# A hybrid decoder step: first tile's queries from PSUM, two of a tile's five low parts on VectorE

## The reference, cut to what matters

```python
def block(xb):                                     # xb: normalised tokens
    q = (xb @ w_query).reshape(PEER_BLOCK, PEER_HEADS, 2, PEER_HALF)      # 8 heads
    s = jnp.einsum('bhpd,phnd->bhpn', q, sub_keys)                        # 128 keys, twice
    top_s, top_i = lax.top_k(s, PEER_TOPK)                                # 16 of 128
    cand = top_s[:, :, 0, :, None] + top_s[:, :, 1, None, :]
    best_s, best_j = lax.top_k(cand.reshape(PEER_BLOCK, PEER_HEADS, PEER_TOPK * PEER_TOPK), PEER_TOPK)
    e1 = jnp.take_along_axis(top_i[:, :, 0, :], best_j // PEER_TOPK, axis=-1)
    e2 = jnp.take_along_axis(top_i[:, :, 1, :], best_j % PEER_TOPK, axis=-1)
    gate = jax.nn.softmax(best_s, axis=-1)
    u_sel = expert_u[e1 * PEER_NKEYS + e2]         # 128 experts of 16384 a token
    act = jax.nn.gelu(jnp.einsum('bd,bhkd->bhk', xb, u_sel), approximate=False)
    v_sel = expert_v[e1 * PEER_NKEYS + e2]
    return jnp.einsum('bhk,bhkd->bd', gate * act, v_sel)
```

## Time and profile before

| | |
|---|---|
| median of three timed runs | 3597.07 us |
| the profiled execution | 3595.11 us, its span 3593.4 us |
| PE busy | 3406.2 us (95%) |
| DVE busy | 2622.7 us (73%) |
| ACT busy | 1017.6 us |
| POOL busy | 1028.0 us |
| TensorE's mean granted clock | 0.968 |

### The profile page before, as it was taken

One profiled execution on the slowest core, in us unless ns is written; L12 is line 12 of the kernel. 1 busy time (PEld: TensorE's weight loads), 2 busy tenths in 40 slices (PEclk: granted clock), 3 DMA queues, 4 the chain that ended last, 5 costly groups with the idle time before them and its releaser, 6 DMA issues.

```text
span 3593.4 us, 57482 instructions
## 1 busy us (share of the span) xinstructions
PE 3406.2 (95%) x21552; PEld 3338.8 (93%) x21552; DVE 2622.7 (73%) x4997; ACT 1017.6 (28%) x1345; POOL 1028.0 (29%) x792
## 2 busy tenths in 40 slices
PE   6989999899998999998899899999999999999997
PEld 6989999879998999998898899999999999999996
DVE  5544344323343179999999899999999999999996
ACT  5742222121232133222454122222222222222222
POOL 0000000000000032222000555555555555555550
PEclk8999999889999999999999999999999999999998
DMA  2111111111232233332689989998999999999993
GB/s 106 35 34 37 47 39 37 49 47 47 90 111 67 89 111 113 103 97 87 194 266 266 362 322 337 331 326 319 325 330 328 336 329 324 323 324 328 332 321 111
DMA packets 304487, 699.12 MB, mean 195 GB/s; under 512 B 23872, under 2 KB 124224, under 8 KB 303328
## 3 DMA queue, kind: packets, MB, share of 16 engines
q0 software_dynamic: 98736, 363.50, 27.8%
q1 hardware_dynamic: 104112, 276.89, 22.8%
q10 hardware_dynamic: 101504, 56.89, 5.2%
HBM read 604.96 MB, written 92.22 MB: 194 GB/s over the span
## 4 chain that ended last, share of the span: by engine, by line
PE 75%; DVE 19%; DMA 2%; issue 1%; ACT 1%; DVEq 1%; ACTq 0%; SPq 0%; POOL 0%; PEldq 0%; POOLq 0%
PE PS L1429 28%; PE PS L366 16%; PE PS L1412 14%; PE PS L1144 7%; PE PS L1173 5%; DVE HOTG L1913 3%; DVE fold L1840 2%; PE PS L381 1%; DVE HOT L1909 1%; DVE HOT L1910 1%; DVE besti L1784 1%; DVE sc L1775 1%; DVE besti L1776 1%; PE PS L1352 1%; DVE best L1781 1%
## 5 line engine op out<-in xcount | busy, mean ns | idle before, releaser
L1429 PE MATMUL PS<-AH,VH 128*128 128x368 f32 x2048 | 514.9, 333 | 18.4 <-DVE AL L2014 12.6
L1429 PE MATMUL PS<-AH,VL 128*128 128x368 f32 x2048 | 515.9, 333 | 0.0
L710 POOL DMA_INDIRECT SLOT<-rows_u,EID x256 | 345.6, 1350 | 580.4 <-DMA GW<-gate_matrices 275.7
L1429 PE MATMUL PS<-AL,VH 128*128 128x368 f32 x2048 | 510.2, 330 | 0.0
L710 POOL DMA_INDIRECT SLOT<-rows_v,EID x256 | 334.4, 1306 | 204.9 <-DVE SLOT L1946 166.7
L1429 PEld LDWEIGHTS PS<-AH,VH 128*128 128x128 f32 x2048 | 366.0, 189 | 21.1 <-DVE AL L2014 13.8
L1429 PEld LDWEIGHTS PS<-AL,VH 128*128 128x128 f32 x2048 | 367.0, 189 | 0.0
L1429 PEld LDWEIGHTS PS<-AH,VL 128*128 128x128 f32 x2048 | 366.2, 189 | 0.0
L1955 DVE SCALAR_TENSOR_TENSOR XLF<-SLOT,GA,XLF 128x1024 f32<-128x1024 f32 x256 | 327.4, 1279 | 0.8 <-DMA SLOT<-rows_v,EID 0.5
L1030 ACT ACTIVATE VH<-VRAW 128x512 fp32r<-128x512 f32 x256 | 157.6, 628 | 565.0 <-PE PS L1429 565.0
L1946 DVE SCALAR_TENSOR_TENSOR SLOT<-SLOT,XHF 128x1024 f32<-128x1024 f32 x256 | 311.7, 1218 | 5.4 <-DMA SLOT<-rows_u,EID 5.1
(11 more groups left out here) (331 smaller groups left out, 6703.9 us busy)
## 6 DMA issues: line engine op xcount, KB each, us to landing
RAW<-experts_u SPq DMA_DIRECT2D x128, 512.0 KB, 6.1
VRAW<-experts_v SPq DMA_DIRECT2D x256, 256.0 KB, 5.8
gate_matrices<-stg ACTq DMA_DIRECT2D x22, 2048.0 KB, 10.3
GW<-gate_matrices SPq DMA_DIRECT2D x96, 384.0 KB, 6.9
RAW<-weights SPq DMA_DIRECT2D x69, 512.0 KB, 3.5
activations<-AS SPq DMA_DIRECT2D x64, 368.0 KB, 2.5
AS<-activations SPq DMA_DIRECT2D x64, 368.0 KB, 3.0
GW<-gate_matrices SPq DMA_DIRECT2D x32, 320.0 KB, 5.8
```

The source lines that it names most:

```text
L710: pool.indirect_dma_start(out=SLOT[n % NSLOT][:, :], out_offset=None, in_=table, in_offset=bass.IndirectOffsetOnAxis(ap=ids, axis=0)).then ...
L1429: mm = pe.matmul(PS[:, 4 + 2 * (d % 2) + t, 0:CH], w[:, d % 2, c * P:c * P + P], x[:, c, t * CH:t * CH + CH], start=(c == 0 and n == 0), s ...
```

## The change

1. `SEL_E`: tile 0 has 4 early blocks and tile 7 has 5 (before 5 and 4). The sum stays 44.
2. In the query projection ScalarE copies, for each of 8 heads, the first 128 columns from PSUM to `qst`, ahead of the copy to `qrow`. The first DMA into `qst` goes away.
3. TensorE transposes only `xtok(0)` first (into banks 6 and 7), then makes the scores of tile 0, then block 0. `xtok(1)` follows after block 2 and `XS` after block `FIRST_E[1]`, both by way of banks 0 and 1.
4. The zeroing of the two accumulators goes from VectorE to ScalarE (an activation with scale 0).
5. The low parts: of the blocks of tile i+1, the first two are made by VectorE in the lookups of tile i (after L1845 and after L1854). The others stay on GpSimd, and the first of these three now waits until VectorE has finished tile i. The DMA of the queries of tile i+1 stands behind that one.

```diff
-SEL_E = (5, 5, 5, 5, 5, 5, 5, 4, 5)
+SEL_E = (4, 5, 5, 5, 5, 5, 5, 5, 5)
...
-            for b in range(2):
-                pool.wait_ge(q_out[b], 16 * (HP // 2))
-            pool.dma_start(qst[:, :, :], q_dram[:, :, 0:P]).then_inc(qst_in, 16)
...
             def e_low(n, slot):
 
+                pool.wait_ge(e_lo, n)
                 pool.wait_ge(e_hi, n + 1)
...
+            e_low(0, 0)
             pool.iota(IOTA[:, :, :], pattern=[[1, NKEYS], [0, 2]], base=0, channel_multiplier=0,
                       allow_small_or_imprecise_dtypes=True).then_inc(iota_set, 1)
-            for n in range(PRE + 1):
+            for b in range(2):
+                pool.wait_ge(q_out[b], 16 * (HP // 2))
+            for n in range(1, PRE + 2):
                 e_low(n, n % 2)
             for i in range(NTILE):
-                e_low(FIRST_E[i] + 1, (FIRST_E[i] + 1) % 2)
+                if 0 < i <= NSP + 1:
+                    pool.wait_ge(sel_done, i + 1)
+                elif i:
+                    pool.wait_ge(sel_g, i - NSP - 1)
+                e_low(FIRST_E[i] + 2, FIRST_E[i] % 2)
                 if i + 1 < NTILE:
                     pool.wait_ge(sel_mm, i + 1)
...
-                for r in range(2, SEL_E[i] + 1):
+                for r in range(3, SEL_E[i]):
                     e_low(FIRST_E[i] + r, (FIRST_E[i] + r) % 2)
...
                 act.wait_ge(unit_done, filled(unit_of(n)))
+                act.activation(qst[:, j, :], PS[:, 3 * (n % 2), 0:P], ACT.Copy)
                 act.activation(thirds(qrow[:, j % 2, :]), pset(n % 2), ACT.Copy).then_inc(free_w, 1)
...
-            for b in range(NSP):
-                act.activation(xtok(b), wide(b), ACT.Copy).then_inc(tok_set, 1)
-            act.activation(XS, PS[:, 6:8, :].rearrange("p a (k t) -> p (a k) t", t=HALF), ACT.Copy).then_inc(tok_set, 1)
-            e_block(0, 0, 16)
+            act.activation(xtok(0), wide(3), ACT.Copy).then_inc(tok_set, 1)
             act.wait_ge(sel_mm, 1)
             sel_scores()
+            e_block(0, 0, 16)
             e_block(1, 1, 16)
...
                     e_block(n, n % 2, 16 * (n // 2 + 1))
+                    if r == 0 and i == 0:
+                        act.wait_ge(tok_mm, 2)
+                        act.activation(xtok(1), wide(0), ACT.Copy).then_inc(tok_set, 1)
+                        for b in range(NSP):
+                            act.activation(acc(b), C[:, 0:D].rearrange("p (k t) -> p k t", k=KD), ACT.Copy, scale=0.0
+                                           ).then_inc(tok_set, 1)
+                    if r == 0 and i == 1:
+                        act.wait_ge(tok_mm, 3)
+                        act.activation(XS, PS[:, 0:2, :].rearrange("p a (k t) -> p (a k) t", t=HALF), ACT.Copy
+                                       ).then_inc(tok_set, 1)
...
             pe.wait_ge(free_w, HP + 2)
             pe.drain().then_inc(e_mm, 2)
-            x_transposes()
+            x_transposes(0, 6)
+            sel_scores(0)
             e_block(0, 0)
-            pe.wait_ge(tok_set, NSP + 1)
-            sel_scores(0)
+            pe.wait_ge(tok_set, 1)
             e_block(1, 1)
...
+                    if r == 0 and i == 0:
+                        pe.wait_ge(sel_sc, 1)
+                        x_transposes(1, 0)
+                    if r == 0 and i == 1:
+                        pe.wait_ge(sel_sc, 2)
+                        half_transposes()
...
                 dve.tensor_tensor(hot[:, :, :, :], places(topf), names(startb), ALU.is_ge)
+                e_low(FIRST_E[i + 1])
                 dve.drain()
...
                 dve.tensor_tensor(hot[:, :, :, :], places(topf), names(iota_b), ALU.is_equal)
+                if i + 1 < NTILE:
+                    e_low(FIRST_E[i + 1] + 1)
                 dve.drain()
...
-            dve.wait_ge(tok_mm, 1)
-            for b in range(NSP):
-                dve.memset(acc(b), 0.0)
```

More of the change, by code:

```diff
@@ L1322, in sel_scores @@
             def sel_scores(n):
-                pe.wait_ge(qst_in, 16 * n + 32)
+                pe.wait_ge(qst_in, 16 * n + 16)
                 for h in range(HP):
@@ L1327, in sel_scores, with x_transposes, half_transposes @@
                 mm.then_inc(sel_mm, 1)
-            def x_transposes():
-                for b in range(NSP):
[L1333 to L1336, removed]
+            def x_transposes(b, at_bank):
+                for k in range(KD):
+                    out = PS[:, at_bank + k // 4, (k % 4) * P:(k % 4) * P + P]
+                    pe.matmul(out, XH[:, k, b * P:b * P + P].bitcast(F32), const("ident"), start=True, stop=False)
+                    mm = pe.matmul(out, XL[:, k, b * P:b * P + P].bitcast(F32), const("ident"), start=False, stop=True)
+                mm.then_inc(tok_mm, 1)
+            def half_transposes():
                 for k in range(KD):
                     for h in range(2):
-                        out = PS[h * HALF:h * HALF + HALF, 6 + k // 4, (k % 4) * P:(k % 4) * P + P]
+                        out = PS[h * HALF:h * HALF + HALF, k // 4, (k % 4) * P:(k % 4) * P + P]
                         for n, x in enumerate((XH, XL)):
@@ L1377, in _ @@
                         pe.wait_ge(sel_sc, i + 1)
+                        if i < 2:
+                            pe.wait_ge(tok_set, 2 + 3 * i)
                         if i - 1 > NSP:
@@ L1449, in flush_half @@
             def flush_half():
-                pe.wait_ge(tok_set, NSP + 2)
+                pe.wait_ge(tok_set, NSP + 4)
                 for k in range(KD):
@@ L1749, in _, with e_low @@
                 split_lo(dve, B_WQ + j + 2, (B_WQ + j + 1) % 2)
+            def e_low(m):
+                dve.wait_ge(e_lo, m)
+                dve.wait_ge(e_hi, m + 1)
+                dve.tensor_tensor(WL[:, m % 2, :], RAW[:, m % 2, :], WH[:, m % 2, :].bitcast(F32),
+                                  ALU.subtract).then_inc(e_lo, 1)
             def evict(i):
@@ L1962, in _ @@
                 s_gated(0, e)
-            dve.wait_ge(tok_set, NSP + 1)
+            dve.wait_ge(tok_set, NSP + 3)
             def group_dve(g, first=False, last=False):
@@ L2032, in group_dve @@
                     if last and d == 2:
-                        dve.wait_ge(tok_mm, 2)
+                        dve.wait_ge(tok_mm, 4)
                         for b in range(NSP):
```

9 lines of the change are left out of this document (3 added, 6 removed).

## The result

| | before | after |
|---|---|---|
| median of five timed runs | 3597.85 us | 3617.77 us |
| the profiled execution | 3595.11 us | 3618.53 us |
| VectorE's first tile | 1283.34 | 1270.44 |
| the gate matrices begin | 1724.81 | 1748.66 |

The changed kernel is slower: ratio 1.0053, 95% interval 1.0041 to 1.0064. (The median before of 3597.07, given further up, is of three of these five runs.) The prediction said 3617 us, in a range of 3602 to 3632, so the forecast case came in. The span grew by 23.4 us (3593.4 to 3616.8) and the gate matrices begin 23.85 later, so nothing behind this stage gave time back or took more.

The account below looks back on a forecast made before the run. TensorE and VectorE were both taken as close to the bound. 13 us late by tile 4, +7.6 in tiles 4 to 7 and +0.5 in tile 8 made 21 on 3595.1, forecast as a median of 3617 us, range 3602 to 3632.

Parts of the forecast that it names:

- Shift of the gate matrices = shift of the end: After the tiles: any shift of the gate matrices' start, 1724.81 before, was taken as an equal shift of the end.
- The copies of queries, 0.4: Query projection: eight 128-column copies on ScalarE were charged 0.4 us in all, bounds 0 and 2.5.
- Tile 0's start, 15.1 earlier: VectorE's first tile was to start at 1268.2, 15.1 us earlier than at 1283.34.
- The wait at the first low part, 23 us: Tile 0: VectorE was to stand 23 us at its first low part, for block 4's chain through TensorE and ScalarE.
- c: Time the granted clock costs TensorE's scores after idle time: between 0 and 2.5 us, taken as 1.2 a start.
- Tile 1: VectorE was to stall 6.6 us, after 3.2 us of TensorE idle time; tile 2 would start 10 us late.
- Tiles 2 and 3, 50 each: Same chain holds VectorE 2 to 4 us each: 50 us a tile against 48.1, 13 late at tile 4.
- Tiles 4 to 7, 51.9 each: Scores wait for the eviction, VectorE then for ScalarE's high part: 51.9 us a tile against 50.0, +7.6 for four.
- rival (b): TensorE's clock does not fall after idle time: sum about +8 or +5, 3602 us; chance 0.14.
- the clock that falls at every start: Rival: TensorE starts cold after each wait, 3.3 us more at 7 or 8 starts, 3630 us; chance 0.15.
- Low parts in VectorE's maxima hold nobody: GpSimd's low parts beside VectorE's maxima were assumed to hold neither engine; if they collided, 2 us a tile.
- Rival (c), faster, 3575: Collisions go and VectorE's low parts never wait: 44 us less at best, half if engines wait a little, 3575; chance 0.13.

Follow-up runs that it names:

- The early tile alone: Changed kernel with every low part on GpSimd and five blocks in tile 0, as before: 3580.07 us, ratio 0.9946; timed again 3579.07 us, ratio 0.9942.
- The filler matmuls: Changed kernel plus 14 unused 128-column matmuls on TensorE ahead of the scores of tiles 5 to 8: 3611.97 us, ratio 1.0031.
- the best kernel here: Changed kernel with low parts and block shares as before, and the exponential one early block later from tile 3 on: 3573.10 us, ratio 0.9925.

## Why the prediction was right

**Shift of the gate matrices = shift of the end.** It held: 23.85 and 23.4. Of the 23.85, the stage itself is 21.2, the predicted 21; the other 2.6 arise before it. Of these, 2.5 stand before ScalarE's first copy to `qrow` (1183.63 before, 1186.11 after), where the code is the same; in all profiled executions that copy began at 1182.82 to 1186.86, so I put them down to variation between runs. This also means that the median landing within 1 us of 3617 is better than the method deserves. The prediction's own working, 3595.1 + 21 and the 2 us to the median, gives 3618 and not 3617.

**The copies of queries, 0.4.** TensorE's waits for them grew from 1.36 to 1.53 and from 1.96 to 2.1 us: 0.3. From the first copy to `qrow` to the first transpose it was 74.9 us in the three kernels without the copies and 75.1 in the changed kernel's trace; of the nine others with them three show 75.1 and six 76.6. So the copies cost 0.2 here and can cost 1.7, within the bounds given.

**Tile 0's start, 15.1 earlier.** 12.9 by the clock, 15.5 against TensorE's first transpose (24.8 us from it before, 9.2 after).

**The wait at the first low part, 23 us.** 23.95, by the links that the prediction named: low part, queries, scores, block 4, Gelu, table, exponential, high part. The idle time of TensorE in it was 3.0 and not 4.1, and c was 1.6 (4.95 for the scores) and not 1.2. The early tile alone, which keeps the lead, shows that nothing else in the change eats it.

**Tile 1.** Predicted stall 6.6, measured 6.96; predicted idle time ahead of the scores 3.2, measured 2.66. Tile 1 took 51.9, predicted 51.3 (1336.0 + 1.2 to 1388.5).

**Tiles 2 and 3, 50 each.** 49.9 and 47.8: the second is 2 us shorter than I allowed. The lag at tile 4 is 13.7, of which 2.6 stood before the stage: 11.1, for a predicted 13.

**Tiles 4 to 7, 51.9 each.** 52.7. VectorE's first low part waited 7.0, 8.1, 6.9 and 3.7 us, where 4 to 7 were forecast. Here a term was mis-sized: c. I took 1.2 from two rows of the kernel before, in which 3.89 us of idle time cost 2.5 and 2.62 cost nothing. The same stretch has a third such row, which I did not read:

```profile
1588.18 5.38 PE L1325 MATMUL PS<-KEYS,qst 128*128 128x256 f32 x16 [2.28 <-issue]
1593.21 0.68 PE L1352 MATMUL PS<-XH,WH 128*128 128x368 f32 x2
```

Here 2.28 us of idle time, less than in the row that cost nothing, cost 1.7 (5.03 for the scores, granted clock 0.66). The mean of the three is 1.4, and rival (b)'s support, that idle times under 3 us cost nothing, was already gone. The filler matmuls measured 1.7 on the mean, and without them the tile would be 51.0, close to the 50.7 that the prediction gave for c = 0. With c = 1.7 its sum for the tile is 52.4. Tile 8, predicted 0.5 longer than before, was 0.7 shorter (49.2 for 49.9). So the errors, 1.9 us too much before tile 4, 3.3 too little in tiles 4 to 7 and 1.2 too much in tile 8, cancel: that the stage comes to 21.2 for a predicted 21 is in part luck.

The Trainium skill's rule of the clock that falls at every start ("TensorE: Matmul & The Clock Gate", "HAM oscillation — how this bites in real kernels") would give scores of 6.6 us each. The six rows of the changed kernel with over 2 us of idle time ahead say 4.95, 5.03, 5.03, 6.09, 4.84 and 3.35: the trace agrees in part, and the measurement decides at just under half of the rule's price, 1.5 of 3.3 us on the mean.

**Low parts in VectorE's maxima hold nobody.** They don't. The first maxima of tile 5 and the low part beside them, VectorE's first:

```profile
1541.31 3.18 DVE L1804 MAX8 best<-sc 128x8 f32<-128x128 f32 x16
...
1541.24 2.39 POOL L680 TENSOR_TENSOR WL<-RAW,WH 128x1024 fp32r<-128x1024 f32 x1 [19.65 <-DVE gate L1900]
```

The 16 maxima take 3.18 us together. One by one, a MAX8 of this shape takes 0.28 us (median), with a GpSimd instruction under way or without. And `pick<-hot,delta` (L1847 before, L1880 after) takes 1.22 or 1.23 in all nine tiles; before it took 3.21 to 3.27 in seven of them. Counting VectorE's single instructions of over 1.9 us, each of which had a low part beside it, gives 27 before and one after. This part of the change did what it says: 27 collisions of 2.0 us are 54, and the busy time shows 32.1 less with 20.8 of low parts added, which is 52.9. What it bought was spent at the waits.

**Rival (c), faster, 3575.** Its time is nearly that of the best kernel here, but by another way. It asked that TensorE finish block FIRST_E[i+1] - 2 within 26 us of the tile's start; in tile 4 it finished 34.6 us in (ScalarE goes on at 1523.22), where the forecast had 33.7. What the prediction did not price is that the first part of the change alone gives 20.6 us, nearly all of the 22 in (c).

## What to carry to other kernels

When two engines are both near their bound, count an instruction moved from one queue to another by what it must wait for, and not by its duration: here the move of 17 low parts of 1.23 us removed some 53 us of collisions and brought 68 us of waits. A lead on one engine is kept only as long as nothing in its queue is bound to the slower one, so test the parts of a change apart: the early start alone is worth 20.6 us, and was lost to a part that came with it. When a hand-written order places a short step (here an exponential), its best place depends on which engine leads at that point, tile by tile.

## What the runs showed of the hardware

```profile
1310.57 2.73 DVE L1868 TENSOR_TENSOR fold<-pick 128x1024 f16<-128x1024 f16 x1
...
1309.51 3.24 POOL L680 TENSOR_TENSOR WL<-RAW,WH 128x1024 fp32r<-128x1024 f32 x1 [8.08 <-ACT WH L955]
```

  The fold takes 0.69 alone and ends here at 1313.3, after the low part (1312.75). The low part itself takes 3.24 instead of 2.4: it came while VectorE's `pick` (1309.27 to 1310.5) was under way. This agrees with the Trainium skill, "SBUF — State Buffer", "SBUF: two separate sides", where whichever starts first holds the shared port for the whole instruction. MAX8 was not held (0.28 us with and without).
- TensorE's clock after a short idle time. In the kernel before, scores of 3.35 us took 5.86, 5.03 and 3.34 after 3.89, 2.28 and 2.62 us of idle time; in the changed kernel 4.95, 5.03, 5.03, 6.09, 4.84 and 3.35 after 3.02, 2.66, 3.68, 4.06, 4.06 and 2.53. The length of the idle time alone does not tell the price: 2.28 cost 1.7 and 2.62 nothing, and 4.06 cost 2.7 once and 1.5 once. What does, these runs do not show. Idle times of 0.8 to 1.0 us cost nothing (3.34, both kernels). Fourteen small matmuls in the idle time brought the scores to 3.37, and the stretch's granted clock from 0.94 or 0.97 to 1.00.
- The moment at which ScalarE first copies to `qrow`, behind code that is the same in all of these kernels, varied by 4.0 us between profiled executions (1182.82 to 1186.86). The stage's start varied by 4.5 (1257.75 to 1262.28), which holds the copies of queries as well. Kernels were therefore compared within the stage.
